# Rounding remainders of eight norms moved to GpSimd, three norms' squares summed whole, new order of the steps

## The chip, the cores and the metric

One Trainium2 chip, one core. The metric is the device time of one execution in microseconds. Five engines take part: TensorE (PE: matmuls, and its weight loads, PEld), VectorE (DVE), ScalarE (ACT), GpSimd (POOL) and SyncE (SP, which starts nearly all DMAs). Each works through its own list of instructions in order; semaphores tie them together.

## The reference

Two layers of a decoder with 528 tokens (16 learned ones and 512 of the input) of width 1024, in fp32. A layer is

```
a = rms_norm(h); proj = a @ w_in                    # columns for three groups of heads
DSA: q, k normed and rotated; an indexer's scores choose 128 keys per query; softmax over them
FoX: q, k normed; softmax of q k / 8 + c_q - c_k, c the running sum of log sigmoid of a gate
GLA: gated linear attention; decay from log_sigmoid((glr @ w2 + b)) / 16, summed in chunks;
     its output normed per head, times silu(gg)
h += concat(DSA, FoX, GLA) @ w_out
h += (silu(gate) * up) @ w_down, with gate, up = rms_norm(h) @ w_gate_up
```

`rms_norm(y) = y * rsqrt(mean(y*y) + eps) * gain`, over 64 or (GLA's output) 128 features. Features lie on the partitions here, so the sum of squares over a head is a product with a matrix of ones on PE.

## The kernel before

All products with weights are made from rounded halves: a weight unit (128 x 1024) comes by DMA to `raw`, ACT rounds it to `whi` (line 1099), POOL makes the remainder `wlo` (line 604), and PE adds whi*xhi, whi*xlo (lines 716, 807, 808) and wlo*xhi (lines 722, 813, the low pass). Each layer has 24 projection units, 8 of the output, 44 of gate and up, 24 of the way down.

While PE works on the 24 projection units, all engines also do the mixers. A step is one piece of this: `("proj", k, hf, p)` is a third of one half of unit k (DKIK, IQ, SMALL, DQ, FQ, FK, FV, GQ, GK, GV, GG name the units; p = 0 and 1 are the high passes over four tiles each, p = 2 is the low pass); `square` and `norm` with a unit are the two stages of a norm; `index`, `lowest`, `topk` and `select` choose the keys; `logits`, `turn`, `values`, `back`, `mixed` are attention for a group, a block and a head; `gla_att`, `gla_kv`, `gla_out` are the chunks of GLA. Steps of one kind have a fixed order among themselves (`chains_of_steps`). How the kinds are interleaved on each engine is written out by hand: `STEPS_OF` has a string of letters per layer and engine (A is a projection, B prenorm, C square, D norm, and so on), and `BANKS_OF` says in which of four PSUM banks each of PE's side jobs lies. An engine never takes steps in another order than its string, whatever is ready.

A norm of unit k goes so. ACT squares the features twice: whole to `sqb` (line 1166) and rounded to `sq_parts[:, 1]` (line 1167). DVE subtracts one from the other to `sq_parts[:, 0]` (line 1457), the remainder. PE multiplies both parts by ones, four matmuls of 266 columns (line 823). ACT makes Ln and Exp of the sums (lines 1139, 1175), DVE scales the features (lines 1445, 1448). The first seven norms (DKIK, DQ, DQ+1, FQ, FQ+1, FK, FK+1) come early in the mixers, the four of GLA's output (GV to GV+3) late. There is one set of square tiles, so ACT squares the next only when the sums of the last are made:

```
if n:
    wait_done(("norm", NORM_ORDER[n - 1]))
```

The gate of GLA is one step on DVE, `gate_log` (line 1487 on): one combination, ten running sums of a chunk each (line 1493), then the exponents' arguments. `turn_tile` of SMALL (line 846) transposes a unit for the heads. In layer 1 PE's first pieces (all of DKIK, and of IQ) are made ahead of the mixers' steps by `first_halves`, which leaves them out of the list. At the mixers' end `out` adds up the first output units: part 0 the GLA half, part 1 the attention half (line 716).

## Time and profile before

| | us |
|---|---|
| median of 3 runs | 1332.86 (1332.19 to 1334.34) |
| profiled execution | 1333.27 |
| its span | 1331.5 |
| PE busy | 1308.7 (98%) |
| DVE busy | 649.2 (49%) |
| ACT busy | 539.7 (41%) |
| POOL busy | 530.9 (40%) |

The span counts from the first instruction to the last; the execution's time has some 1.8 us around it. Busy time of PE is drawn with modelled ends that overlap the next matmul's start, so short waits do not show as idle time. The mixers of layer 0 lie between 25 and 256 us, those of layer 1 between 697 and 914 us.

### The profile page before, as it was taken

How to read it: one execution, taken by the hardware profiler on the slowest of the kernel's cores; microseconds unless marked ns; L12 is line 12 of the kernel's file. 1: busy time of each engine (PE TensorE's matmuls, PEld its weight loads, DVE VectorE, ACT ScalarE, POOL GpSimd, SP SyncE). 2: the span in 40 equal slices, each digit the busy share in tenths (PEclk: the TensorE clock that was granted, in tenths of full speed). 3: DMA queues.
4: the chain of work that ended last, by engine and by line, in shares of the span. 5: the costliest groups of instructions: out<-in, count | busy, mean ns of one | idle time of the engine just before them, and what ended most of it. 6: DMA issues, size and time to landing. Idle time of an engine off the chain costs nothing.

```text
span 1331.5 us, 22884 instructions
## 1 busy us (share of the span) xinstructions
PE 1308.7 (98%) x8678; PEld 1195.7 (90%) x8678; DVE 649.2 (49%) x1108; ACT 539.7 (41%) x874; POOL 530.9 (40%) x256
## 2 busy tenths in 40 slices
PE   7999999999999999999999999999999999999998
PEld 7999999999999999999998899987878888888887
DVE  4688988563333333322225999985643333331000
ACT  5566458543222222322235674385332222222221
POOL 2535311234444434444436342112444444444444
PEclk9999999999999999999999999999999999999999
DMA  5221210132222222222323212111222322223334
GB/s 185 89 81 55 80 33 32 33 111 80 95 94 79 94 95 81 92 95 98 106 80 94 80 67 67 33 48 48 95 83 93 94 94 94 95 95 104 102 99 153
DMA packets 33595, 114.11 MB, mean 86 GB/s; under 512 B 4352, under 2 KB 4736, under 8 KB 33536
## 3 DMA queue, kind: packets, MB, share of 16 engines
q1 hardware_dynamic: 32816, 112.23, 25.5%
q10 hardware_dynamic: 720, 1.09, 0.2%
q8 instruction: 38, 0.62, 0.2%
q14 instruction: 21, 0.17, 0.0%
HBM read 109.84 MB, written 2.10 MB: 84 GB/s over the span
## 4 chain that ended last, share of the span: by engine, by line
PE 52%; issue 32%; POOL 9%; DVE 5%; ACT 1%; DMA 1%; POOLq 0%; SPq 0%; DVEq 0%; ACTq 0%
PE ps L716 20%; PE ps L722 10%; POOL wlo L604 9%; PE ps L813 5%; PE ps L807 5%; PE ps L808 4%; PE ps L930 1%; PE ps L878 1%; PE ps L903 1%; PE ps L823 1%; PE ps L913 1%; PE ps L987 1%; DMA raw<-in_weights 1%; PE ps L773 1%; PE ps L969 1%
## 5 line engine op out<-in xcount | busy, mean ns | idle before, releaser
L604 POOL TENSOR_TENSOR wlo<-raw,whi 128x1024 fp32r<-128x1024 f32 x202 | 501.1, 2482 | 789.9 <-ACT whi L1099 789.6
L1099 ACT ACTIVATE whi<-raw 128x1024 fp32r<-128x1024 f32 x202 | 213.9, 1059 | 587.5 <-PE ps L722 549.1
L716 PE MATMUL ps<-xhi,whi 128*128 128x264 f32 (+1 forms) x1096 | 327.9, 322 | 7.2 <-ACT whi L1099 7.1
L716 PE MATMUL ps<-xlo,whi 128*128 128x264 f32 (+1 forms) x1096 | 326.6, 322 | 0.0
L716 PEld LDWEIGHTS ps<-xhi,whi 128*128 128x128 f32 x1096 | 206.8, 189 | 24.4 <-ACT whi L1099 6.8
L716 PEld LDWEIGHTS ps<-xlo,whi 128*128 128x128 f32 x1096 | 206.7, 189 | 16.1
L722 PE MATMUL ps<-xhi,wlo 128*128 128x264 f32 (+1 forms) x1096 | 195.4, 321 | 0.3 <-POOL wlo L604 0.2
L722 PEld LDWEIGHTS ps<-xhi,wlo 128*128 128x128 f32 x1096 | 162.9, 188 | 17.3 <-issue 1.0
L807 PE MATMUL ps<-xhi,whi 128*128 128x264 f32 (+1 forms) x632 | 176.3, 308 | 0.4 <-ACT whi L1099 0.3
L808 PE MATMUL ps<-xlo,whi 128*128 128x264 f32 (+1 forms) x632 | 171.1, 300 | 0.0
L716 PE MATMUL ps<-hlo,whi 128*128 128x264 f32 (+1 forms) x528 | 157.3, 321 | 0.0
L716 PE MATMUL ps<-hhi,whi 128*128 128x264 f32 (+1 forms) x528 | 157.2, 321 | 0.0
L1711 DVE TENSOR_TENSOR hid<-ps,rstd 128x528 f32<-128x528 f32 (+1 forms) x44 | 30.8, 700 | 213.1 <-PE ps L722 213.1
L807 PEld LDWEIGHTS ps<-xhi,whi 128*128 128x128 f32 x632 | 119.1, 188 | 5.6 <-issue 0.8
L808 PEld LDWEIGHTS ps<-xlo,whi 128*128 128x128 f32 x632 | 119.2, 189 | 3.5
L1726 DVE TENSOR_TENSOR h<-ps,h 128x528 f32<-128x528 f32 (+1 forms) x16 | 11.2, 700 | 204.3 <-PE ps L722 204.3
L716 PEld LDWEIGHTS ps<-hlo,whi 128*128 128x128 f32 x528 | 99.3, 188 | 7.9
L716 PEld LDWEIGHTS ps<-hhi,whi 128*128 128x128 f32 x528 | 99.2, 188 | 7.8
L1717 DVE TENSOR_TENSOR hlo<-hid,hhi 128x528 f32 (+1 forms) x44 | 82.9, 1883 | 41.1 <-ACT hhi L1372 41.1
L813 PE MATMUL ps<-xhi,wlo 128*128 128x264 f32 (+1 forms) x632 | 102.5, 304 | 0.0
L722 PE MATMUL ps<-hhi,wlo 128*128 128x264 f32 (+1 forms) x528 | 95.5, 321 | 0.0
L813 PEld LDWEIGHTS ps<-xhi,wlo 128*128 128x128 f32 x632 | 87.0, 188 | 4.3 <-issue 0.8
(196 smaller groups left out, 1696.1 us busy)
## 6 DMA issues: line engine op xcount, KB each, us to landing
raw<-in_weights SPq DMA_DIRECT2D x202, 512.0 KB, 3.5
out_hT<-h SPq DMA_DIRECT2D x8, 256.0 KB, 4.2
h<-in_hT SPq DMA_DIRECT2D x4, 264.0 KB, 6.4
h<-in_hT ACTq DMA_DIRECT2D x4, 264.0 KB, 6.0
cst<-in_consts SPq DMA_DIRECT2D x1, 780.5 KB, 9.3
xnb<-feat SPq DMA_DIRECT2D x20, 33.2 KB, 2.2
feat<-xnb SPq DMA_DIRECT2D x20, 33.2 KB, 2.0
cst<-in_consts SPq DMA_DIRECT2D x1, 532.0 KB, 4.5
```

Source lines behind the costliest of these rows:

```text
L604: nc.gpsimd.tensor_tensor(wlo[:, b], raw[:, b], whi[:, b].bitcast(F32), ALU.subtract).then_inc(split_done, 1)
L716: nc.tensor.matmul(bank(bank_no, cut.stop - cut.start), whi[:, b, k % KT], x(k)[t][:, cut], start=(first and k == ks[0] and t == 0), stop= ...
L722: ins = nc.tensor.matmul(bank(bank_no, cut.stop - cut.start), wlo[:, b, k % KT], x(k)[0][:, cut], start=False, stop=(last and k == ks[-1]))
L773: ins = nc.tensor.matmul(bank(b0 + hf, CUT), ones, square[:, cut], start=(k == 0), stop=(k == KT - 1))
L807: nc.tensor.matmul(o, whi[:, k % 2, n], xhi[:, n, cut], start=(n == 0), stop=False)
L808: nc.tensor.matmul(o, whi[:, k % 2, n], xlo[:, n, cut], start=False, stop=False)
L813: ins = nc.tensor.matmul(o, wlo[:, k % 2, n], xhi[:, n, cut], start=False, stop=(n == KT - 1))
L823: ins = nc.tensor.matmul(bank(b0 + hf, HALF), ones_r[:, at:at + 128], sq_parts[:, part, hf * HALF:(hf + 1) * HALF], start=(part == 0), sto ...
L878: ins = nc.tensor.matmul(ps[out_rows, at + a:at + z], q, kk[:, 2 * m + part, a:z], start=(part == 0), stop=(part == 1))
L1099: return nc.scalar.activation(whi[:, b], raw[:, b], ACT.Copy).then_inc(hi_done, 1)
L1711: nc.vector.tensor_tensor(tokens(l, hid[:, b]), wide(l, 4 * b + 2), tokens(l, rstd[:]), ALU.mult).then_inc(ev.acc_free, 1)
L1717: nc.vector.tensor_tensor(hlo[:, bass.ds(j * 2 + b, 1), of].rearrange("p a t -> p (a t)"), hid[:, b, of], hhi[:, bass.ds(j * 2 + b, 1), of ...
```

## The change

1. The norms of DKIK, DQ and DQ+1 keep one whole square in `sqb` (two tiles in turn) and PE sums it as plain fp32: two matmuls of 266 columns per norm, no rounded square, no remainder. ACT may square one norm ahead there.
2. For the other eight norms the remainder is made by POOL, with its own steps `square_parts` in POOL's list, between the weight units' subtractions; DVE has no square step any more.
3. `gate_log` is cut into `gate_log`, `gate_sum` (twice) and `gate_arg`, so that other steps can stand between them.
4. All strings of `STEPS_OF` and `BANKS_OF` are new, the DMA list's too.

```diff
+SPLIT_SQUARES = (FQ, FQ + 1, FK, FK + 1, GV, GV + 1, GV + 2, GV + 3)
...
+def square_step(k):
+    return ("square_parts" if k in SPLIT_SQUARES else "square", k)
...
-        "square": [("square", k) for k in NORM_ORDER],
+        "square": [square_step(k) for k in NORM_ORDER],
...
-        "gate": [("gate", 0), ("gate", 1), ("gate_log",), ("gate_exp",), ("decays",), ("turn_k", 0), ("turn_k", 1)],
+        "gate": [("gate", 0), ("gate", 1), ("gate_log",), ("gate_sum", 0), ("gate_sum", 1), ("gate_arg",),
+                 ("gate_exp",), ("decays",), ("turn_k", 0), ("turn_k", 1)],
...
-     POOLE: "AAQQAAAAAAAAAAQQQAAAAQAAAAAAAA",
...
+     POOLE: "AAQQAAAACACAQCAQACAQAAAAAQAAAAACCCCAAA",
...
+                def square(k):
+
+                    pool.wait_ge(ev.sq_whole, SPLIT_SQUARES.index(k) + 1)
+                    pool.wait_ge(ev.sq_ready, SQUARES[k] + 1)
+                    nc.gpsimd.tensor_tensor(sq_parts[:, 0], sqb[:, 0], sq_parts[:, 1].bitcast(F32), ALU.subtract).then_inc(ev.sq_split, 1)
...
-                    pe.wait_ge(ev.sq_split, SQUARES[k] + 1)
                     at = C_BLK - C_ONE if k < GV else 0
+                    if k in SPLIT_SQUARES:
+                        pe.wait_ge(ev.sq_split, SPLIT_SQUARES.index(k) + 1)
+                    else:
+                        pe.wait_ge(ev.sq_ready, SQUARES[k] + 1)
                     for hf in range(2):
-                        for part in range(2):
-                            ins = nc.tensor.matmul(bank(b0 + hf, HALF), ones_r[:, at:at + 128],
-                                                   sq_parts[:, part, hf * HALF:(hf + 1) * HALF], start=(part == 0), stop=(part == 1))
+                        half = slice(hf * HALF, (hf + 1) * HALF)
+                        if k in SPLIT_SQUARES:
+                            for part in range(2):
+                                ins = nc.tensor.matmul(bank(b0 + hf, HALF), ones_r[:, at:at + 128], sq_parts[:, part, half],
+                                                       start=(part == 0), stop=(part == 1))
+                        else:
+                            ins = nc.tensor.matmul(bank(b0 + hf, HALF), ones_r[:, at:at + 128].bitcast(F32),
+                                                   sqb[:, SQUARES[k] % 2, half], start=True, stop=True)
...
-                    if n:
+                    if k in SPLIT_SQUARES or n and NORM_ORDER[n - 1] in SPLIT_SQUARES:
                         wait_done(("norm", NORM_ORDER[n - 1]))
-                    elif l == 0:
+                    elif n >= 2:
+                        wait_done(("norm", NORM_ORDER[n - 2]))
+                    elif n == 0 and l == 0:
 
                         act.wait_ge(cst_loaded, 16)
                         act.wait_ge(ones_loaded, 16)
                         nc.scalar.activation(ones_r[:], cst[:, C_ONE:C_ROT], ACT.Copy).then_inc(ones_rounded, 1)
-                    nc.scalar.activation(sqb[:, 0], feat[:, place(k)], ACT.Square).then_inc(ev.sq_whole, 1)
-                    nc.scalar.activation(sq_parts[:, 1], feat[:, place(k)], ACT.Square).then_inc(ev.sq_ready, 1)
+                    if k in SPLIT_SQUARES:
+                        nc.scalar.activation(sqb[:, 0], feat[:, place(k)], ACT.Square).then_inc(ev.sq_whole, 1)
+                        nc.scalar.activation(sq_parts[:, 1], feat[:, place(k)], ACT.Square).then_inc(ev.sq_ready, 1)
+                    else:
+                        nc.scalar.activation(sqb[:, n % 2], feat[:, place(k)], ACT.Square).then_inc(ev.sq_ready, 1)
...
-                def square(k):
-                    n = SQUARES[k]
-                    dve.wait_ge(ev.sq_whole, n + 1)
-                    dve.wait_ge(ev.sq_ready, n + 1)
-                    nc.vector.tensor_tensor(sq_parts[:, 0], sqb[:, 0], sq_parts[:, 1].bitcast(F32), ALU.subtract).then_inc(ev.sq_split, 1)
...
-                    for t in range(2):
-                        for c in range(NB):
-
-                            of = feat[:, place(GG + 2 + t), block_of(c)]
-                            own[0] += 1
-                            nc.vector.tensor_tensor_scan(feat[:, place(GG + t), block_of(c)], of, of, 0.0, ALU.add,
-                                                         ALU.min).then_inc(ev.dve_step, 1)
+
+                def gate_sum(t):
+                    for c in range(NB):
+
+                        of = feat[:, place(GG + 2 + t), block_of(c)]
+                        own[0] += 1
+                        nc.vector.tensor_tensor_scan(feat[:, place(GG + t), block_of(c)], of, of, 0.0, ALU.add, ALU.min).then_inc(ev.dve_step, 1)
                     dve.wait_ge(ev.dve_step, own[0])
-                    b = chunks(e)
+
+                def gate_arg():
+                    b = chunks(feat[:, pair(GG)])
                     mid, end = b[:, :, :, BLK // 2 - 1], b[:, :, :, BLK - 1]
```

The order of instructions moves everywhere in the mixers. Three places:

POOL in layer 0, in the first half of the mixers; `wlo<-raw,whi` is a weight unit's remainder, `sq_parts` a norm's. Before:

```order
18 L623 COPY q_odd<-cst 4x532 x2
19 L604 TENSOR_TENSOR wlo<-raw,whi 128x1024 x10
20 L663 COPY k_fox<-feat 4x532 x4
21 L669 MEMSET feat 64x1064
22 L623 COPY feat<-cst 4x532 x2
23 L676 MEMSET feat 64x1064
24 L604 TENSOR_TENSOR wlo<-raw,whi 128x1024 x4
```

Now:

```order
18 L631 COPY q_odd<-cst 4x532 x2
19 L612 TENSOR_TENSOR wlo<-raw,whi 128x1024 x4
20 L695 TENSOR_TENSOR sq_parts<-sqb,sq_parts 128x532
21 L612 TENSOR_TENSOR wlo<-raw,whi 128x1024
22 L695 TENSOR_TENSOR sq_parts<-sqb,sq_parts 128x532
23 L612 TENSOR_TENSOR wlo<-raw,whi 128x1024
24 L671 COPY k_fox<-feat 4x532 x4
25 L695 TENSOR_TENSOR sq_parts<-sqb,sq_parts 128x532
26 L612 TENSOR_TENSOR wlo<-raw,whi 128x1024
27 L677 MEMSET feat 64x1064
28 L631 COPY feat<-cst 4x532 x2
29 L612 TENSOR_TENSOR wlo<-raw,whi 128x1024
```

The FoX remainders now stand one by one between the weight units; those of GLA come later, four in a row ahead of the last three units of the layer's projections (in layer 1 with one unit behind the first of them).

PE in layer 1, from the sums of norm GV+1 to those of norm GV+2 (`ps<-sq_parts` a norm's sums, `v_fox,probs_t` a head's values, `cst,probs` a head's transposes, `xhi,wlo` a low pass). Before:

```order
2405 L823 MATMUL ps<-sq_parts,ones_r 128x266 x4
2406 L945 MATMUL ps<-v_meta,p_meta_t 128x260
2407 L938 MATMUL ps<-cst,p_meta 128x128
2408 L813 MATMUL ps<-xhi,wlo 128x512 x8
2409 L930 MATMUL ps<-v_fox,probs_t 128x65 x3
2410 L913 MATMUL ps<-cst,probs 128x128 x3
2411 L930 MATMUL ps<-v_fox,probs_t 128x65 x3
2412 L913 MATMUL ps<-cst,probs 128x128 x3
2413 L823 MATMUL ps<-sq_parts,ones_r 128x266 x4
```

Now:

```order
2381 L842 MATMUL ps<-sq_parts,ones_r 128x266 x4
2382 L960 MATMUL ps<-cst,p_meta 128x128
2383 L952 MATMUL ps<-v_fox,probs_t 128x65 x3
2384 L935 MATMUL ps<-cst,probs 128x128 x3
2385 L952 MATMUL ps<-v_fox,probs_t 128x65 x3
2386 L827 MATMUL ps<-xhi,wlo 128x512 x8
2387 L842 MATMUL ps<-sq_parts,ones_r 128x266 x4
```

One head's transposes and the meta tokens' values have gone from between the two norms. A plain fp32 matmul (values, meta values) appears as two records in the trace, so that a row x3 makes six; a transpose and a matmul of rounded operands appear as one.

PE at the end of layer 1's mixers (`v_fox,probs_t` the last head's values, `v_meta` the meta tokens' part, `cst,o_tok` the transposes of finished heads, `mix_hi,whi` the output projection). Before:

```order
2460 L930 MATMUL ps<-v_fox,probs_t 128x65 x8
2461 L945 MATMUL ps<-v_meta,p_meta_t 128x260
2462 L954 MATMUL ps<-cst,o_tok 128x128 x2
2463 L716 MATMUL ps<-mix_hi,whi 128x512
2464 L716 MATMUL ps<-mix_lo,whi 128x512
```

Now:

```order
2472 L730 MATMUL ps<-mix_hi,whi 128x512
2473 L730 MATMUL ps<-mix_lo,whi 128x512
2474 L736 MATMUL ps<-mix_hi,wlo 128x512 x4
2475 L976 MATMUL ps<-cst,o_tok 128x128 x2
2476 L730 MATMUL ps<-mix_hi,whi 128x512
```

The last transposes have moved from ahead of the GLA half of the output projection to behind it (rows 2457 to 2474 of the new list), directly ahead of the attention half.

## Rows read from the trace of the kernel before

**Rows 1.** page, span and busy time of the engines
```profile
span 1331.5 us, 22884 instructions
PE 1308.7 (98%) x8678; PEld 1195.7 (90%) x8678; DVE 649.2 (49%) x1108; ACT 539.7 (41%) x874; POOL 530.9 (40%) x256
```

**Rows 2.** windows: mixers 0, output and feed-forward 0, mixers 1: length, busy us (count), clock
```profile
core 0: us, PE busy (x) PEld busy (x) DVE busy (x) ACT busy (x) POOL busy (x), PEclk, DMA share, GB/s
25.00:256.00 231.00, 225.46 (x1794) 216.50 (x1793) 183.96 (x432) 139.28 (x283) 76.12 (x49) 1.00 0.18 59
256.00:697.00 441.00, 440.72 (x3585) 439.13 (x3584) 149.72 (x143) 131.03 (x160) 187.79 (x76) 1.00 0.28 92
697.00:914.00 217.00, 211.29 (x1431) 190.68 (x1430) 179.75 (x397) 136.84 (x273) 74.23 (x49) 1.00 0.19 62
```

**Rows 3.** waits of PE, whole run: us in total, times, longest
```profile
PE ps L823 <- DVE sq_parts L1457: 4.8, 5, 1.2
PE ps L846 <- DVE feat L1435: 1.4, 2, 1.1
PE ps L716 <- DVE mix_lo L1635: 1.1, 1, 1.1
PE ps L954 <- DVE o_tok L1626: 1.0, 1, 1.0
```

**Rows 4.** timeline of PE: start, us, engine, line, what [idle before]
```profile
45.19 0.74 PE L846 MATMUL ps<-cst,feat 128*128 128x128 f32 x5 [1.06 <-DVE feat L1435]
...
57.42 0.74 PE L823 MATMUL ps<-sq_parts,ones_r 128*128 128x266 f32 x4 [0.55 <-DVE sq_parts L1457]
...
73.09 0.28 PE L808 MATMUL ps<-xlo,whi 128*128 128x264 f32 x1
74.56 0.73 PE L823 MATMUL ps<-sq_parts,ones_r 128*128 128x266 f32 x4 [1.18 <-DVE sq_parts L1457]
...
698.54 0.74 PE L823 MATMUL ps<-sq_parts,ones_r 128*128 128x266 f32 x4 [0.79 <-DVE sq_parts L1457]
...
733.12 0.73 PE L823 MATMUL ps<-sq_parts,ones_r 128*128 128x266 f32 x4 [1.22 <-DVE sq_parts L1457]
```

**Rows 5.** timeline of ACT and DVE ahead of two of these starts
```profile
69.21 0.64 ACT L1167 ACTIVATE sq_parts<-feat 128x532 fp32r<-128x532 f32 x1
73.70 0.71 DVE L1457 TENSOR_TENSOR sq_parts<-sqb,sq_parts 128x532 fp32r<-128x532 f32 x1
...
696.39 0.65 ACT L1166 ACTIVATE sqb<-feat 128x532 f32<-128x532 f32 x1 [0.98 <-DVE feat L1435]
697.68 0.71 DVE L1457 TENSOR_TENSOR sq_parts<-sqb,sq_parts 128x532 fp32r<-128x532 f32 x1 [1.32 <-ACT sq_parts L1167]
```

**Rows 6.** groups by form: busy us, mean ns of one, idle before
```profile
L1457 DVE TENSOR_TENSOR sq_parts<-sqb,sq_parts 128x532 fp32r<-128x532 f32 x22 | 16.7, 759 | 5.6 <-ACT sq_parts L1167 5.3
L604 POOL TENSOR_TENSOR wlo<-raw,whi 128x1024 fp32r<-128x1024 f32 x202 | 501.1, 2482 | 789.9 <-ACT whi L1099 789.6
```

**Rows 7.** timeline of PE: a norm's sums, and one head's fp32 logits
```profile
25.91 0.73 PE L823 MATMUL ps<-sq_parts,ones_r 128*128 128x266 f32 x4
26.48 0.29 PE L807 MATMUL ps<-xhi,whi 128*128 128x264 f32 x1
...
905.41 1.05 PE L903 MATMUL ps<-k_fox,q_odd 128*128 128x264 f32 x4
906.30 0.60 PE L913 MATMUL ps<-cst,probs 128*128 128x128 f32 x4
```

**Rows 8.** timeline of DVE and POOL, 41 to 47 us
```profile
41.91 2.79 DVE L1467 TENSOR_TENSOR xnb<-xnb 96x532 f32<-96x532 f32 x1
41.39 5.54 POOL L604 TENSOR_TENSOR wlo<-raw,whi 128x1024 fp32r<-128x1024 f32 x2
```

**Rows 9.** timeline, a GLA norm's sums and the next squares
```profile
203.79 0.74 PE L823 MATMUL ps<-sq_parts,ones_r 128*128 128x266 f32 x4
205.18 0.63 ACT L1167 ACTIVATE sq_parts<-feat 128x532 fp32r<-128x532 f32 x1
```

More of the change, by code:

```diff
@@ L239 @@
+    "23130120320320200203203020302301320",
 )
 ON = {
-    "prenorm": (PE, ACTE), "square": (ACTE, DVEE), "norm": (PE, ACTE, DVEE), "gather": (DMAE,),
-    "rope": (PE, DVEE), "spread": (DMAE,), "split_k": (ACTE, DVEE), "split_q": (ACTE, DVEE), "part": (ACTE,),
-    "even_q": (ACTE,), "turn_tile": (PE, ACTE), "index": (PE, ACTE, DVEE), "lowest": (DVEE,),
-    "select": (DVEE,), "topk": (DVEE,), "fox_log": (ACTE, DVEE), "gate": (PE, ACTE), "gate_log": (ACTE, DVEE),
+    "prenorm": (PE, ACTE), "square": (ACTE,), "square_parts": (ACTE, POOLE), "norm": (PE, ACTE, DVEE),
@@ L248 @@
+    "gather": (DMAE,), "rope": (PE, DVEE), "spread": (DMAE,), "split_k": (ACTE, DVEE),
+    "split_q": (ACTE, DVEE), "part": (ACTE,), "even_q": (ACTE,), "turn_tile": (PE, ACTE),
+    "index": (PE, ACTE, DVEE), "lowest": (DVEE,), "select": (DVEE,), "topk": (DVEE,), "fox_log": (ACTE, DVEE),
+    "gate": (PE, ACTE), "gate_log": (ACTE, DVEE), "gate_sum": (DVEE,), "gate_arg": (DVEE,),
     "gate_exp": (ACTE,), "decays": (DVEE,), "turn_k": (PE, ACTE), "masks": (POOLE,), "clear_fox": (POOLE,),
@@ L1342, in gla_mix @@
                     nc.scalar.activation(mix_hi[:, 4 + hd], feat[:, place(GG + hd)], ACT.Copy).then_inc(ev.gla_hi, 1)
-                do = dict(prenorm=prenorm, proj=proj, square=square, norm=norm, split_k=split_k, split_q=split_q_hi, part=part, even_q=even_q,
+                do = dict(prenorm=prenorm, proj=proj, square=square, square_parts=square, norm=norm, split_k=split_k, split_q=split_q_hi, part=part, even_q=even_q,
                           turn_tile=turn_tile,
@@ L1684, in gla_lo @@
                                             ALU.subtract).then_inc(ev.gla_split, 1)
-                do = dict(proj=proj, square=square, norm=norm, rope=rope, split_k=split_k, split_q=split_q_lo, gate_log=gate_log, fox_log=fox_log, decays=decays, index=index, topk=topk, lowest=lowest,
+                do = dict(proj=proj, norm=norm, rope=rope, split_k=split_k, split_q=split_q_lo, gate_log=gate_log, gate_sum=gate_sum, gate_arg=gate_arg,
+                          fox_log=fox_log, decays=decays, index=index, topk=topk, lowest=lowest,
                           select=select, logits=logits, scale=scale, mixed=mixed, gla_att=gla_att, gla_kv=gla_kv,
```

47 lines of the change are left out of this document (23 added, 24 removed).

## Prediction

> **What bounds the kernel now.** I read the page's busy shares first: TensorE (PE) is busy for 1308.7 of 1331.5 us, no other engine for more than half [rows 1]. The second view is the table of windows, since the change touches only the mixers [rows 2]. The reader is to see that the output and feed-forward stretch of layer 0 leaves PE 0.3 us idle in 441. The mixers leave 5.5 us in layer 0 (231.00 less 225.46) and 5.7 us in layer 1 (217.00 less 211.29), 11.2 together, while VectorE (DVE) is busy for 80 to 83% of them. The granted clock is 1.00, the 2.4 GHz level, throughout, so it has no term here. So the time can change in two ways: by the work on PE, and by those 11.2 us. Third, the list of PE's waits says what they are made of [rows 3]: five waits of a norm's sums (line 823) for DVE's remainder of line 1457 make 4.8 us, the largest item. The timeline shows three of them at the first three norms: 0.55 us at 57.42 (DQ, layer 0), 0.79 at 698.54 (DKIK, layer 1), 1.22 at 733.12 (DQ+1, layer 1), in sum 2.56 [rows 4]. The other two, 2.24 us, are FOX norms.
>
> A wait costs more than its idle time. At 73.09 the last matmul ahead of a wait starts; the norm starts 1.47 us later with 1.18 idle [rows 4]. Matmuls of this kind start 0.123 us apart (441 us through 3585 [rows 2]), though each is drawn 0.28 long. So the loss is 1.47 - 0.12 = 1.35, the idle time plus 0.16. The five cost 4.8 + 5 x 0.16 = 5.6 us.
>
> Durations come from the profiled execution, 1333.27 us (span 1331.5 and 1.8 around it); the median of the runs shown is 1332.86, 0.41 lower. The sum is made against the first and moved by 0.41 at its end.
>
> **1. The first three norms' squares are summed whole.** They are now plain fp32. PE's price is read from the FOX logits, which are plain fp32 too: line 903 issues two matmuls of 264 columns for a head, the trace draws four records, and they take from 905.41 to 906.30, 0.89 us. A norm's four rounded matmuls take from 25.91 to 26.48, 0.57 us [rows 7]. So each such norm costs 0.32 more, and 3 norms x 2 layers add **+1.9 us** on the engine that sets the time. Off PE go 6 remainders on DVE (6 x 0.76 = 4.6 us [rows 6]) and 6 second squares on ACT.
>
> Do the three waits go? At 698.54 PE had arrived 0.79 earlier, at 697.75. ACT's first square ends at 696.39 + 0.65 = 697.04 [rows 5], and this alone is now waited for: the wait goes. The piece that the new order puts behind this norm instead of ahead (pIQ) is in layer 1 already issued before the mixer's steps begin, so PE arrives no earlier. For DQ and DQ+1 the remainder is no longer behind DVE's queue either. Gain: 2.56 + 3 x 0.16 = **-3.0 us**.
>
> **2. FOX and GLA remainders by GpSimd (POOL).** 16 of them leave DVE (12.2 us) and come to POOL. POOL's subtraction of 1024 columns has a mean of 2.48 us [rows 6]; for 532 columns that makes an estimate of 2.48 x 532/1024 = 1.29 us, against 0.71 undisturbed on DVE. The bounds of a remainder's delay are 0.5 us later by that difference, and earlier by all that it stood in DVE's queue. The row at 74.56 shows how much that is: ACT's second square ended at 69.21 + 0.64 = 69.85, DVE began the remainder at 73.70, 3.85 us later, since the selection's steps stood ahead of it [rows 5]. I take the earlier side for the two FOX waits, because POOL is busy for only a third of the mixers (76 of 231 us [rows 2]) and 3.85 is more than its longer subtraction: **-2.6 us** (2.24 + 2 x 0.16). For the GLA norms I take 0; they show no wait now, and what covers them is told under the second rival.
>
> Each remainder that waits on POOL holds up the weight splits queued behind it. The first extract shows one split between every two FOX remainders. A unit's split is needed only a unit later on PE (48 matmuls, 5.9 us at 0.123), against 1.29 us more for each: cost 0 while that cover stands; without it PE waits at its low pass (line 813).
>
> The Trainium skill, page "SBUF — State Buffer", section "Who interferes with whom", calls the port pair that DVE and GpSimd share an exclusive lock held for a whole instruction. What the trace shows of it goes into the sum by itself: at 41.91 DVE's addition of two SBUF tiles took 2.79 us, while POOL had two subtractions running from 41.39 [rows 8]; undisturbed remainders of like size take 0.71. So the 20.6 us of POOL (16 x 1.29) give part of DVE's relief back. I count the relief of DVE as no gain on PE beyond the waits named.
>
> **3. The steps of the gate** run the same instructions, in three steps instead of one. Their cost is 0; before, ten scans stood in a row on DVE, and now projections' evictions go between them.
>
> **4. The new order.** In layer 0 the turn of SMALL waited 1.06 us for DVE (45.19 [rows 4]); it now comes three pieces later (24 matmuls, 2.9 us), so the wait goes: **-1.2 us**. At layer 1's end the transpose of the last heads waited 1.02 us for DVE [rows 3]. Now the GLA half of the output projection stands between (third extract). But then the attention half follows that transpose directly, as layer 0 has it, where it waited 1.1 us for the last mix_lo [rows 3]: one for the other, 0. All other steps move as well, the gates and projections forward, layer 0's attention back. New waits cannot be read from the old trace. Their bounds are 0 and the 11.2 us that the mixers show now, if the new order were twice as bad; I take **+1.5 us**, nearer to 0, because what is left of 11.2 once the waits named (4.8, 1.06) are gone is spread over small ones. The place that I expect first is FQ's norm in layer 0. It follows the last index queries closely, and two squares on ACT, a 1.29 us remainder and perhaps a running split lie between.
>
> **Sum:** +1.9 - 3.0 - 2.6 - 1.2 + 1.5 = -3.4 us, 1329.9 for a profiled execution, **1329.5 us** as a median. What a measurement of this kernel tells from no change is about 0.2%, 2.7 us.
>
> **Rivals.** *The lock eats the relief (no change).* The Trainium skill, page "Perfetto Trace Analysis", section "Optimizing Scalar/DVE Operations", says that moving work between DVE and GpSimd might not help, because they share an SBUF port. As a mechanism of this kernel: POOL's 20.6 us stand against the 16.7 us of remainders that DVE loses [rows 6]; if each of them stopped DVE, DVE would be 3.9 us slower. The row at 41.91 speaks for it; against it, MAX and MATCH_REPLACE, most of DVE's work in the selection, read one tile each. Then the two FOX waits stay or come back elsewhere (no -2.6) and half of the 3.9 reaches PE: +1.9 - 3.0 - 1.2 + 1.5 + 1.9 = +1.1, a median of 1334.0.
>
> *The GLA norms starve (slower).* They are a chain: sums on PE, two squares on ACT, the remainder, the next sums. From the start of one norm's sums to the end of the second square are 2.02 us (203.79 to 205.18 + 0.63 [rows 9]), with 1.29 and 0.2 for hand-overs 3.5 us. In layer 1, between GV+1 and GV+2, the second extract leaves PE 24 records, at a mean of 0.152 (217 us through 1431 [rows 2]) 3.6 us, and the norm's own 0.57: some 0.7 us of cover. A split running on POOL (2.4 us), a DVE operation holding the port, or late squares use it up, and all steps behind the norm wait on PE. If each of the eight GLA norms came 1.2 us after its cover, that is 8 x 1.36 = 10.9 us in place of the 1.5: +6.0, a median of 1338.9. It decides from 7.6 us of new waits on (4.9 gained above, and 2.7). Against it: before, the same norms had no wait, and POOL's splits are sparse there.
>
> *The change does not do what it says:* the waits for remainders were DVE's lateness in general and show up at the next wait on DVE. Then only +1.9 is sure and the rest is exchanged: 1332 to 1335.
>
> **How the numbers follow.** The forecast has 0.50, the lock 0.28, the starving GLA norms 0.17, the exchange 0.05. The forecast's own range is 1325.5 (new waits 0 and 2.5 us more of the small waits gone by DVE's relief: -4.9 - 2.5) to 1331.5. The 8 in 10 range reaches over the second case and leaves out most of the third and the best luck: 1325.5 to 1335.5. Faster by over 0.2% (under 1330.2): 0.50. Within: 0.33. Slower: 0.17.
>
> **What would show it.** Right: in the list of PE's waits no entry of the first three norms, FOX norms under 0.5 us each, PE idle in the two mixers at 7 to 9 us instead of 11.2, fp32 sums of about 0.89 us per norm, and POOL remainders of 1.2 to 1.4 us. Wrong: PE waiting for POOL's sq_parts in the GLA stretch (third case); DVE's two-input operations longer than now, with its busy time down by less than 10 us (second case); a low pass of a projection waiting for wlo (the cover of part 2). The forecast falls if the mixers' PE idle stays at 11 us or more.

## Result: slower, 1336.82 us, and the profile after

The changed kernel takes 1336.82 us in the median of 9 runs (1334.77 to 1338.72), beside 1332.78 for the kernel before (9 runs, same chip): ratio 1.0027, 95% interval [1.0019, 1.0035], so 4.0 us slower, beyond the 2.7 us that I called measurable. The profiled execution took 1338.72 us, 5.45 more than that of before. The page after, against [rows 1]:

```profile
span 1336.9 us, 22872 instructions
PE 1315.5 (98%) x8678; PEld 1202.0 (90%) x8678; DVE 636.8 (48%) x1086; ACT 537.0 (40%) x868; POOL 549.9 (41%) x272
...
PEclk9989999999999999999999999999999999999999
```

DVE has 12.4 us less work and POOL 19.0 more, as the change says. The new thing is in the line of the granted clock: its third slice is an 8. The windows that answer [rows 2] say where:

```profile
25.00:256.00 231.00, 227.57 (x1760) 217.19 (x1759) 176.86 (x419) 137.16 (x280) 83.09 (x57) 0.98 0.17 56
256.00:697.00 441.00, 439.70 (x3587) 438.44 (x3586) 149.76 (x143) 129.42 (x157) 188.64 (x77) 1.00 0.28 93
697.00:914.00 217.00, 212.24 (x1428) 192.76 (x1427) 172.47 (x383) 135.43 (x267) 85.03 (x57) 1.00 0.18 61
```

PE's idle time seems to go from 11.2 to 8.2 us (3.43 and 4.76), inside my 7 to 9. But both mixers now end later, and the wait at the end of each has slipped out of its window:

```profile
260.12 0.36 PE L730 MATMUL ps<-mix_hi,whi 128*128 128x264 f32 x1 [1.02 <-DVE mix_lo L1655]
...
924.67 0.49 PE L730 MATMUL ps<-mix_hi,whi 128*128 128x512 f32 x1 [0.93 <-DVE mix_lo L1655]
```

With these two the bracketed waits of PE's timeline from 25 us on come to 10.1 us (3.37 + 1.02 + 4.76 + 0.93), beside 10.8 before (5.27 + 5.57): 0.8 less, not 3. And PE's busy time in layer 0 rose by 2.1 us while 34 fewer matmuls lie in the window. In windows of 2 us (length, busy us of PE, its weight loads, DVE, ACT and POOL with counts, then the clock):

```profile
84.00:86.00 2.00, 2.00 (x19) 2.00 (x17) 1.93 (x3) 0.39 (x1) 0.51 (x1) 1.00 0.00 0
86.00:88.00 2.00, 1.30 (x6) 0.66 (x4) 1.90 (x7) 1.32 (x3) 1.88 (x3) 1.00 0.00 0
88.00:90.00 2.00, 1.14 (x8) 1.03 (x8) 1.90 (x7) 1.95 (x3) 1.86 (x3) 1.00 0.00 0
90.00:92.00 2.00, 1.82 (x10) 1.75 (x10) 1.86 (x7) 1.84 (x3) 2.00 (x2) 0.66 0.03 8
92.00:94.00 2.00, 2.00 (x8) 1.54 (x8) 1.90 (x5) 0.66 (x2) 1.88 (x3) 0.50 0.30 47
...
98.00:100.00 2.00, 2.00 (x11) 2.00 (x11) 1.45 (x5) 1.97 (x2) 1.03 (x1) 0.50 0.57 168
100.00:102.00 2.00, 2.00 (x15) 2.00 (x15) 0.11 (x1) 1.35 (x3) 0.00 (x0) 0.78 0.23 94
102.00:104.00 2.00, 2.00 (x19) 2.00 (x18) 1.93 (x5) 0.00 (x0) 0.00 (x0) 1.00 0.00 0
```

From 90 to 102 us the mean clock is 0.66, four times 0.50 and 0.78: PE runs at 1.2 GHz instead of 2.4. The work missing is 2 x (0.34 + 4 x 0.50 + 0.22) = **5.1 us**. The matmul of the output projection that waits for the last mix_lo, at the end of the mixers of layer 0, starts at 254.62 us before and at 260.12 after: 5.5 later. From there to the end of the span it is 1076.9 and 1076.8 us. So all of the loss lies in layer 0, and nearly all of it is this stretch. Ahead of it, PE's timeline:

```profile
85.08 1.13 PE L827 MATMUL ps<-xhi,wlo 128*128 128x264 f32 x8
86.14 1.16 PE L888 MATMUL ps<-feat,par_all 16*128 16x266 f32 x4
88.86 0.39 PE L821 MATMUL ps<-xhi,whi 128*128 128x264 f32 x1 [1.56 <-ACT whi L1121]
...
90.28 0.93 PE L842 MATMUL ps<-sq_parts,ones_r 128*128 128x266 f32 x4 [0.18 <-POOL sq_parts L695]
91.01 0.42 PE L821 MATMUL ps<-xhi,whi 128*128 128x264 f32 x1
91.23 0.42 PE L822 MATMUL ps<-xlo,whi 128*128 128x264 f32 x1
```

The gate's product (line 888: four narrow matmuls, 16 rows), a gap of 1.56 us, eight matmuls, and then matmuls start 0.22 us apart instead of 0.12. The gap is a wait for ACT to round the weights of FV. Why ACT is late is read back along three engines (POOL, then DVE, then ACT):

```profile
76.59 1.40 POOL L695 TENSOR_TENSOR sq_parts<-sqb,sq_parts 128x532 fp32r<-128x532 f32 x1 [5.46 <-ACT sq_parts L1192]
77.95 2.46 POOL L612 TENSOR_TENSOR wlo<-raw,whi 128x1024 fp32r<-128x1024 f32 x1
85.50 3.23 POOL L671 COPY k_fox<-feat 4x532 f32<-4x532 f32 x4 [5.08 <-issue]
88.81 1.33 POOL L695 TENSOR_TENSOR sq_parts<-sqb,sq_parts 128x532 fp32r<-128x532 f32 x1
```

```profile
76.43 0.37 DVE L1608 SCALAR_TENSOR_TENSOR score<-score,top 128x144 f32<-128x144 f32 x1
76.83 1.33 DVE L1609 SCALAR_TENSOR_TENSOR score<-score,top 128x144 f32<-128x144 f32 x1
78.19 2.38 DVE L1610 SCALAR_TENSOR_TENSOR score<-score,causal 128x144 f32<-128x144 f32 x1
...
86.21 0.77 DVE L1462 TENSOR_TENSOR feat<-ps,rstd 128x264 f32<-128x264 f32 x2
```

```profile
86.68 0.65 ACT L1191 ACTIVATE sqb<-feat 128x532 f32<-128x532 f32 x1 [2.29 <-DVE feat L1462]
87.23 0.63 ACT L1192 ACTIVATE sq_parts<-feat 128x532 fp32r<-128x532 f32 x1
87.77 1.04 ACT L1121 ACTIVATE whi<-raw 128x1024 fp32r<-128x1024 f32 x1
```

POOL's remainder and the weight split right behind it hold two small DVE operations for 1.33 and 2.38 us; the one ahead of them, of the same shape, took 0.37. In layer 1 the second of them took 0.31 undisturbed. That is 3 us of DVE, of which some 2 are new: the eight DVE instructions of this select took 3.45 us in the kernel before (70.22 to 73.67), one of them stretched to 1.14 us beside a weight split, and take 5.63 here (74.94 to 80.57). DVE then takes unit FK.1 out of PSUM only at 86.21, behind a top-k round, the forget gate's logs and norm FQ1. ACT's squares of FK wait 2.29 us for it, and the rounding of FV's weights stands behind those squares. So the first theory was **clock**: a gap of PE's work brings the fall, and this chain brings the gap. Its rivals: the **price of the edits** (they cost this wherever they stand), and the **order** (the new order loses on PE whatever the clock does).

### The profile page after: what moved, and what is told of

Same layout as the page of the kernel before. It is cut to its first block, busy times and chain, and to the rows that moved or that the text cites. A ratio compares the mean times of both kernels' runs of the same rounds, so it can differ in the third digit from the quotient of the medians.

```text
span 1336.9 us, 22872 instructions
## 1 busy us (share of the span) xinstructions
PE 1315.5 (98%) x8678; PEld 1202.0 (90%) x8678; DVE 636.8 (48%) x1086; ACT 537.0 (40%) x868; POOL 549.9 (41%) x272
## 4 chain that ended last, share of the span: by engine, by line
PE 51%; issue 31%; POOL 9%; DVE 6%; ACT 1%; DMA 1%; POOLq 0%; SPq 0%; DVEq 0%; ACTq 0%
PE ps L730 20%; PE ps L736 10%; POOL wlo L612 9%; PE ps L821 4%; PE ps L827 4%; PE ps L822 4%; PE ps L952 1%; PE ps L900 1%; PE ps L925 1%; PE ps L935 1%; DVE score L1569 1%; PE ps L787 1%; DMA raw<-in_weights 1%; PE ps L1009 1%; DVE feat L1472 1%
## 5 line engine op out<-in xcount | busy, mean ns | idle before, releaser
L1747 DVE TENSOR_TENSOR h<-ps,h 128x528 f32<-128x528 f32 (+1 forms) x16 | 11.2, 699 | 204.3 <-PE ps L736 204.3
```

## The experiments

Orders are given by step names; pFK.1c is the last piece of FK's second weight unit (on ACT the rounding of the unit two further on, on DVE the taking out of PSUM, on POOL a weight split). Each time is a median beside the kernel before on the same chip, whose medians were 1332.97 to 1333.32.

### 1. Two links of the chain, one at a time

```diff
 e1: after, ACT, layer 0
-square_parts:FK  pFK.1c
+pFK.1c  square_parts:FK
 e2: after, DVE, layer 0
-topk:2,0  fox_log  norm:FQ1  pFK.1c
+pFK.1c  topk:2,0  fox_log  norm:FQ1
```

> The changed kernel with one pair of ScalarE steps exchanged in layer 0: the rounding of unit FV's weights goes ahead of the squares of norm FK, so that it does not stand behind DVE's late sum of unit FK.1. In the changed kernel's trace TensorE waits 1.56 us for this rounding at 88.9 us and the granted clock is then 0.50 from 92 to 100 us and 0.66 and 0.78 beside that, about 10 us at 1.2 GHz that cost some 5 us. Theory 'clock': TensorE's gap at 86 to 89 us shrinks, the stretch at 1.2 GHz goes or shrinks, the mean clock comes out at 0.998 to 1.000 instead of 0.996, and the time falls by 3 to 5.5 us to 1331 to 1334. Rival 'price of the edits' (whole fp32 sums and GpSimd's slower remainders cost the time wherever they stand): the time stays within 1 us of 1336.8. Rival 'order': PE loses the time at other waits, and the clock's dip only moves to another place: 1335 to 1338 with the clock still 0.996.

> The same gap attacked from its other end: the changed kernel with DVE's sum of unit FK.1 ahead of the first top-k round (and so ahead of the forget gate's log and norm FQ1's apply, which it stood behind until 86.2 us although TensorE had ended the unit near 80.3). ScalarE's squares of FK then no longer wait for it, and neither does the rounding of FV behind them. Theory 'clock': the same gain as in the run with ScalarE's pair exchanged, 3 to 5.5 us, with a mean clock of 0.998 to 1.000; norm FQ1's apply comes up to 1 us later, which may cost up to 0.5. Rival 'price of the edits': within 1 us of 1336.8. If only one of the two runs recovers the clock, the gap has a second cause than the chain from DVE's sum over the squares to the rounding.

Measured: 1338.57 us (ratio 1.0033 [1.0021, 1.0045]), clock 0.996, and 1339.06 (1.0042 [1.0029, 1.0056]), 0.995. Neither recovers anything. In e1 the wait for the rounding is gone, and at the next norm stands another:

```profile
90.40 0.93 PE L842 MATMUL ps<-sq_parts,ones_r 128*128 128x266 f32 x4 [1.79 <-POOL sq_parts L695]
```

In e2 it is 2.11 us at the same norm FK. The gap has a second cause, which the first had covered: the new order puts POOL's four copies for the forget sums (3.23 us from 85.50, above) ahead of the remainder of FK. That rules out the chain as I had told it, not yet the clock.

### 2. The parts of the change without its order

e3 is the new code with the order and banks of before (gate steps together, remainders on POOL behind the weight splits beside them). e4 is the kernel before with the first three norms summed whole, remainders on DVE. It is not that part quite alone: its code also has the gate in steps, which stand side by side in DVE's list, as in e3. So e3 and e4 differ only in who makes the eight remainders.

```diff
 e4, DVE, both layers
-square:DKIK  square:DQ  square:DQ1
 (the eight others stay)
```

> The changed kernel's code (first three norms' squares summed whole, eleven remainders on GpSimd, the gate's sums in steps) in the order of steps and banks of the kernel before; the remainders stand in GpSimd's order behind the weight step that precedes them in time, and the three gate steps stand together where the one step stood. Theory 'clock and order': the edits themselves are worth -2 to +1 us, so 1331 to 1334 with a clock of 1.00. Rival 'price of the edits': they cost what the changed kernel lost, 1335.5 to 1338. A third possibility is a new wait on GpSimd's remainders, since the old order was not made for them: then PE's idle rows name L842 <-POOL with over 2 us and the time is 1334 to 1337 with the clock at 1.00.

> The kernel before with one part of the change alone: the squares of the first three norms (DKIK, DQ, DQ1) are summed whole in fp32, the other eight remainders stay on DVE where they were, order and banks are those of before. From the prediction: +1.9 us of TensorE for the fp32 sums against -3.0 us of its waits for DVE's remainders, so -1.1 +- 0.7: 1331 to 1332.5. If fp32 sums cost more than the 0.3 us each over the rounded ones, or the wait for DVE is replaced by one for ScalarE's squares, it is 1333 to 1334.5. Theory 'price of the edits' needs at least +1 us here or in the run with GpSimd's remainders in the old order.

Measured: e3 1333.06 (0.9996 [0.9987, 1.0005]); e4 1332.10 (0.9991 [0.9982, 1.0000]). The price of the edits falls as a theory: all of them together cost at most 0.7 us in the old order, by the interval. e4 comes out at -1.2 where -1.1 was forecast for this part; its interval reaches to no change, but its trace agrees, with 8.2 us of bracketed waits in the mixers where the kernel before has 10.8.

### 3. Which layer's order

e8: layer 0 in the old order and banks, layer 1 in the new one.

> The changed code with layer 0 in the old order of steps and banks (as in the run with the old order throughout) and layer 1 in the new one. Theory 'clock': the loss lies in layer 0 alone, so this gives 1331 to 1333.5 (the old order throughout gave 1333.06) with no fall at 90 us; from the idle time in the mixers of layer 1 (4.8 us in the changed kernel, 4.5 in the old order throughout) the new order of layer 1 should be worth nothing or up to +0.5 us. Rival 'order': the new order of layer 1 costs too, 1334.5 or more.

Measured: 1332.63 (1.0000 [0.9991, 1.0009]), clock 1.000 in the profiled execution. The loss is layer 0's order; layer 1's costs nothing in the median. Two of the eleven executions took 1335.40 and 1335.57 at a mean clock of 0.997, so in some of them the clock falls with this order too.

### 4. All waits of that place at once

```diff
 e5: e1, and POOL, layer 0
-pFQ1.1c  spread_sums  square_parts:FK  pFK.1c  clear_even
+pFQ1.1c  square_parts:FK  pFK.1c  spread_sums  clear_even
 e6: e5 and e2
 e11: after, POOL, layer 0: spread_sums, clear_even, clear_gla_even behind pFV1.1c
 e12: e11 and e1 and e2
```

> The changed kernel with both waits of the stretch at 86 to 91 us attacked in one: ScalarE's exchange of the first experiment, and on GpSimd the four copies for the forget sums (3.2 us from 85.5 us) behind the weight step of FK.1 instead of ahead of the remainder of FK. In the first experiment TensorE's wait for the rounding went and one of 1.79 us for that remainder came in its place (GpSimd had the copies in hand until 88.7), the clock fell as before, and the time was 1338.6. Theory 'clock' as it now stands (any gap of some 1.6 to 2.1 us here, next to the gate's small matmuls, is followed by the fall to 1.2 GHz): the wait at norm FK shrinks to 0.7 us or less, the fall goes, mean clock 0.999 to 1.000, time 1331 to 1334. Rival 'order' (the light matmuls of gate and norm at 86 to 91 us bring the fall without any wait): gap small and the clock still falls, 1336 to 1338.

> As the run beside it, and DVE's sum of unit FK.1 ahead of the first top-k round too, so that the squares of FK start some 3 us sooner on ScalarE and GpSimd's remainder is ready before TensorE asks for it. Theory 'clock': no wait over 0.3 us between 86 and 91 us, no fall of the clock, 1331 to 1333.5, not slower than the run beside it. Rival 'order': the clock falls although there is no wait, 1336 to 1338.

Measured: e5 1340.83 (1.0059 [1.0045, 1.0073]), e6 1339.97 (1.0048 [1.0034, 1.0062]). Both miss their numbers, and show where the wait goes. Windows and timeline of e6:

```profile
86.00:88.00 2.00, 2.00 (x12) 1.44 (x11) 1.93 (x5) 1.81 (x4) 1.12 (x1) 1.00 0.00 0
88.00:90.00 2.00, 2.00 (x18) 1.95 (x16) 1.86 (x7) 1.92 (x3) 2.00 (x2) 1.00 0.04 8
90.00:92.00 2.00, 2.00 (x12) 1.48 (x11) 1.86 (x7) 1.36 (x3) 1.81 (x4) 1.00 0.21 39
...
100.00:102.00 2.00, 1.36 (x6) 1.39 (x7) 1.81 (x5) 0.13 (x1) 0.50 (x1) 0.69 0.43 172
102.00:104.00 2.00, 2.00 (x11) 2.00 (x11) 0.66 (x1) 1.97 (x3) 0.00 (x0) 0.50 0.00 0
```

```profile
100.64 1.13 PE L842 MATMUL ps<-sq_parts,ones_r 128*128 128x266 f32 x4 [3.33 <-POOL sq_parts L695]
```

The gate's two products and norm FK pass at 86 to 92 us without a gap, and the clock holds at 1.00. Now PE comes to norm FK1 3.33 us before POOL's remainder, which stands behind the copies and two clears, and the clock falls there. The gap moved and the fall moved with it (in e5: a gap of 3.75 us up to 102.40, in which the clock falls at 101.6).

Both runs, and e2, have a second fall, in layer 1, of 1.7 us by the windows. It begins within 1.4 us of the start of the gate's second product there, ahead of which PE waits 0.51 to 0.52 us. In e6:

```profile
765.00 1.13 PE L888 MATMUL ps<-feat,par_all 16*128 16x266 f32 x4 [0.51 <-DVE stat L1634]
766.00:768.00 2.00, 2.00 (x11) 1.94 (x11) 1.86 (x7) 1.74 (x2) 1.50 (x1) 0.59 0.10 39
```

The profiled executions of the changed kernel and of e1 have the same product at 764.6 to 764.7 with 0.52 and 0.53 us ahead of it, and no fall. So a stretch of this kind can bring the fall and need not.

> The changed kernel with GpSimd's order alone changed in layer 0: the copies for the forget sums and the two clears stand behind the weight step of FV1.1 again, as in the old order, and no longer between the remainders; the remainders of FK and FK1 so come free of them. TensorE's wait for the rounding of FV at 88.9 us (1.56 us, from DVE's late sum through ScalarE's squares) is not touched. Theory 'wait': that gap stays near 1.6 us, so the fall stays, 1335.5 to 1338. If GpSimd's order is the whole cause: clock 1.00 and 1331 to 1334.

> All three waits of layer 0's new order taken away: ScalarE's rounding of FV ahead of the squares of FK, DVE's sum of FK.1 ahead of the first top-k round, and GpSimd's copies and clears behind the weight step of FV1.1. With the first two and the copies only one place later the gap at 89 us was gone, the clock held there, and a new wait of 3.3 us for the remainder of FK1 at 100.6 us brought the fall instead (1339.97). Theory 'wait': no gap over 1.2 us between 75 and 110 us, no fall, mean clock 0.999 to 1.000, time 1331 to 1333.5. Rival 'order': falls again at some other place or PE loses 3 us in small waits, 1335 or more.

Measured: e11 1335.29 (1.0019 [1.0010, 1.0028]), clock 0.998: the gap is 1.55 us as said, and the fall behind it costs 1.7 us by its windows instead of 5.1. e12's profiled execution keeps the clock at 1.000 and takes 1335.67; its other four take 1335.94 to 1338.65, two of them at 0.997, so in some of them the clock falls somewhere, and the median is 1337.90 (1.0035 [1.0021, 1.0048]). I expected 1331 to 1333.5. PE has new waits at other places in e12, the longest 1.67 us for POOL's weight split at 118.36 and 0.98 for a rounding at 114.48. So even without a fall this order is 2.4 us behind (1335.67 against the 1333.27 of before, one execution each), and by e8 the loss is layer 0's: the theory "order" is right for this part.

### 5. What brings the fall

e7 takes the narrow product away and leaves the wait. e9, e10, e13 and e14 put a gap into the kernel **before**, alone: ACT squares DQ n times more, into the same buffer with the same values.

```diff
 e7: after, PE and ACT, layer 0
-gate:0  pFV.0a  norm:FK  pFV.0b  gate:1
+pFV.0a  norm:FK  pFV.0b  gate:0  gate:1
 e9, e10, e13, e14: before, ACT, square(k), n = 2, 3, 4, 6
+if l == 0 and k == DQ:
+    for _ in range(n):
+        own[0] += 1
+        nc.scalar.activation(sqb[:, 0], feat[:, place(k)], ACT.Square).then_inc(ev.act_step, 1)
+        act.wait_ge(ev.act_step, own[0])
 e18: e13, and PE, layer 0: gate:0 right ahead of norm:DQ (ACT's gate:0 behind split_q:2)
```

> The changed kernel with its waits left alone and the first of the gate's two small products (16 rows, 4 matmuls, 1.1 us) moved from ahead of the waited piece to beside the second, behind norm FK. TensorE then reaches the piece of unit FV some 1 us sooner and waits longer for it: a gap of 2 to 2.7 us with full matmuls in front. Theory 'wait' (the idle time brings the fall): the clock falls at 88 to 91 us as before, mean 0.995 to 0.997, 1336 to 1339. Theory 'light work' (the small matmuls beside the gap bring it): the clock stays or its fall is shorter, 1332 to 1335.

Measured: 1339.56 (1.0049 [1.0035, 1.0063]). The gap became 2.67 us at 88.66, with full matmuls ahead of it, and the clock fell (0.50 in 90:92). Narrow work is not needed for that. It fell again at 96.6, behind both of the gate's products, the second with a gap of only 0.80 us ahead of it.

> The kernel before, with one thing added: in layer 0 ScalarE squares DQ two times more (the same values into the same buffer, 0.65 us each) ahead of the two squares that norm DQ needs. Nothing of the output changes. TensorE's wait ahead of norm DQ (0.55 us at 57.4 us in the kernel before) becomes about 1.85 us; there is no gate product or other narrow matmul within some us of it but one pair of 128x144. Theory 'wait': a gap of this length is enough for the granted clock to fall to 1.2 GHz for some 8 to 10 us, so +1.3 us for the wait and +4 to +5 for the clock: 1337 to 1340. Theory 'light work' (it needs the small matmuls beside the gap): +1.3 to +2.5 us only, 1334 to 1336, clock 1.000.

> As the run beside it with three squares more, so a gap of about 2.5 us. Theory 'wait': the fall is there for certain, 1338 to 1341. If the shorter gap brings no fall and this one does, the length of the gap decides; if neither does, idle time alone is not what brings it: 1335 to 1337.

Measured: 1333.82 (1.0004 [0.9994, 1.0014]) and 1334.38 (1.0010 [1.0000, 1.0019]); no fall, but the gaps came out at 0.74 and 1.36 us, not 1.85 and 2.5: the first extra squares were partly hidden, why I did not trace. They decide nothing about 2 us. So two more:

> The kernel before with four more squares of DQ on ScalarE in layer 0 (same values, same buffer) ahead of those that norm DQ needs. Two and three of them made the gap ahead of norm DQ 0.74 and 1.36 us, so some 0.62 us each: about 2.0 us now. Theory 'wait': the fall of the granted clock follows it as it followed the gaps of 1.56 to 3.75 us in the changed order, some 4 us more in time: 1337.5 to 1340, mean clock 0.997. Rival 'wait alone is not enough' (it also takes the narrow gate products or further gaps close by): the time goes on as with two and three squares (1333.8, 1334.4), so 1335 to 1336, clock 1.000.

> As the run beside it with six more squares: a gap of about 3.2 us. Theory 'wait': a fall in every execution, 1339 to 1342, mean clock 0.996 to 0.997. Rival: 1336 to 1337.5 with the clock at 1.000. If this one falls and the run beside it does not, the length from which a gap decides lies between 2.0 and 3.2 us here and is shorter beside the gate.

Measured: e13 1335.72 (1.0019 [1.0010, 1.0028]), e14 1337.81 (1.0034 [1.0023, 1.0045]). First the row of e13 and its window, then those of e14:

```profile
58.37 0.73 PE L823 MATMUL ps<-sq_parts,ones_r 128*128 128x266 f32 x4 [2.10 <-DVE sq_parts L1462]
...
60.00:62.00 2.00, 2.00 (x19) 2.00 (x18) 1.94 (x4) 1.95 (x3) 0.00 (x0) 1.00 0.00 0
```

```profile
60.67 1.22 PE L823 MATMUL ps<-sq_parts,ones_r 128*128 128x266 f32 x4 [3.46 <-DVE sq_parts L1462]
...
60.00:62.00 2.00, 1.33 (x6) 1.36 (x7) 1.85 (x5) 1.72 (x4) 0.00 (x0) 0.52 0.03 8
```

In these executions a gap of 3.46 us alone brings the fall (0.52 in 60:62: it begins at 60.1, in the gap itself) and one of 2.10 does not. Other executions differ: the seven of e14 reach from 1339.38 us at a mean clock of 0.997 to 1335.91 at 1.000, the ten of e13 from 1334.75 at 1.000 to 1337.09 at 0.997. Their mean clock does not say where it fell: the profiled e13, at 0.999, has a fall of 1.7 us at the end of layer 1's mixers (914.9 to 918.3), where nothing was changed. In the changed kernel 1.56 us seems to be enough in nearly every execution: eight of the nine have 0.996 or 0.997, the fastest (1334.77) 0.999. e18 asks whether the gate's product takes part:

> As the run with four more squares of DQ (gap of 2.10 us ahead of norm DQ, no fall of the clock behind it, 1335.7), with the first gate product (4 matmuls of 16 rows, 1.1 us) moved from its place at 117 us to right in front of that norm, so that it stands beside the gap as in the changed kernel (where 1.56 us were enough). It takes some 0.5 to 1 us of the gap's time, so the gap is 1.1 to 1.6 us and the time without a fall 1334.5 to 1336. Theory 'gap and narrow products together': the clock falls at 60 us in most executions, +3 to +5 us: 1338 to 1340, mean clock 0.997. Rival 'the gap alone counts': no fall, since the gap is shorter than the one that brought none, clock 0.999 to 1.000.

Measured: 1338.39 (1.0039 [1.0025, 1.0052]), 2.7 us above e13.

```profile
57.73 1.45 PE L864 MATMUL ps<-feat,par_all 16*128 16x266 f32 x4 [1.41 <-ACT relu L1280]
60.18 1.26 PE L821 MATMUL ps<-sq_parts,ones_r 128*128 128x266 f32 x4 [1.00 <-ACT feat L1222]
58.00:60.00 2.00, 1.18 (x4) 0.39 (x3) 1.85 (x5) 1.95 (x4) 0.00 (x0) 0.62 0.07 29
60.00:62.00 2.00, 1.82 (x8) 1.82 (x9) 1.03 (x2) 0.59 (x2) 0.00 (x0) 0.50 0.03 8
```

The fall is there, with no single gap over 1.41 us. The product waited for its bank, so the idle time is in two parts, 1.41 + 1.00. But the fall does not need the second part: 0.62 in 58:60 with 0.50 behind it puts its start at 60 - 2 x 0.76 = 58.5 us, while the product was running (57.73 to 59.18). Ahead of it lie 1.41 us without work and 0.8 of the narrow product, less idle time than the 2.10 us of e13 that brought no fall. In layer 0 of e6 the same product has no gap beside it and no fall. My reading, which fits these runs and which e18 supports without proving it: what counts is a stretch in which the array has little to do, gaps and narrow products together. What it does not explain is why the same stretch brings the fall in one execution and not in another, as in layer 1 of e6 and e1. That the fall is in part chance in each execution is a rival that e13 and e18 do not exclude, though all five executions of e18 are at 0.997 to 0.999 and the ten of e13 at 0.997 to 1.000.

### 6. The new order with the remainders on DVE

e15: after, with the eight remainders back on DVE, each where ACT's squares should be ready.

> The changed kernel, its order and banks, with the eight remainders of the FoX and GLA norms back on DVE (each put where ScalarE's squares are ready); the whole sums of the first three norms and the gate's steps stay. Theory 'GpSimd' (the new order fails because GpSimd holds the shared port while DVE is due and comes late with remainders): DVE is back in time, the gaps of 86 to 91 us shrink under 1.2 us, no fall, 1331 to 1334. Rival 'order' (TensorE reaches unit FV before DVE and ScalarE are through whatever GpSimd does; DVE has 2.8 us more work in front): the gap stays at 1.5 us or grows, with the fall, 1336 to 1340.

Measured: 1351.25 (1.0146 [1.0130, 1.0161]), far beyond either number. PE waits 2.98 us for the rounding of FV at 90.53 (1.56 in the changed kernel), up to 2.11 for remainders in both layers and 2.79 for another step of DVE at 902.27, with three falls of the clock, 6.8 us by the windows. With the remainders at these places DVE has no room for their 12 us in the new order. How much of the 14 us over the changed kernel is my choice of places, and so whether POOL is needed there, was not tried.

### 7. A version that beats both

e16 and e17 are e4 with two more norms summed whole: FQ1 in layer 0 and FK in layer 1 (e16), FQ in layer 0 and FQ1 in layer 1 (e17).

```diff
 e17
-SPLIT_SQUARES = (FQ, FQ + 1, FK, FK + 1, GV, ...)
+SPLIT_SQUARES = ((FQ + 1, FK, FK + 1, GV, ...),
+                 (FQ, FK, FK + 1, GV, ...))
```

> The kernel with whole squares alone (1332.1) with two more norms summed whole in fp32: FQ1 in layer 0 and FK in layer 1, the two at which TensorE still waits for DVE's remainder (0.70 us at 73.8, 1.06 us at 749.0). By the terms so far +0.33 us each for the fp32 sums, and up to -1.76 for the waits: -1.1 +- 0.6, so 1330.5 to 1331.8. If ScalarE's squares and not the remainders are what is late, the waits stay at half and the time is 1331.8 to 1332.5.

> The kernel with whole squares alone (1332.1), with FQ in layer 0 and FQ1 in layer 1 summed whole too: the trace of the run with FQ1 and FK shows that the waits of 0.70 us at 74.0 and of 1.06 us at 749.8 belong to these two. +0.33 us each for the fp32 sums, -1.76 at most for the waits: -1.1 +- 0.5, so 1330.5 to 1331.6. If it comes out at 1332 to 1333, the waits are gone and the time is lost behind them, at DVE's or ScalarE's steps that TensorE then reaches sooner.

Measured: e16 1332.43 (1.0000 [0.9991, 1.0009]): no gain, and its trace still had both waits, 0.70 and 1.06 us: I had named the wrong norms. e17 **1331.00** (0.9984 [0.9975, 0.9993]), the fastest here: 2.1 us below the kernel before and below the changed one, whose own ratio is 1.0027. Both waits for remainders are gone; the largest entry of PE's list in the mixers is now the turn of SMALL, in both layers:

```profile
PE ps L861 <- DVE feat L1455: 1.9, 2, 1.1
```

## Why the prediction was wrong

Forecast 1329.5, range 1325.5 to 1335.5, with 0.17 for slower; it came out slower and above the range.

**The step that failed** is the sentence "The granted clock is 1.00, the 2.4 GHz level, throughout, so it has no term here." It is true of the kernel before and says nothing of the one after: a new wait costs its own length and, where the clock falls with it, more: 5.1 us here, 1.7 to 5.1 in the experiments. My own sum had new waits of 1.5 us, all at face value. The other terms against the runs: the waits gone and new were to give -3.0 - 2.6 - 1.2 + 1.5 = -5.3 and give -0.8; the fp32 sums were to cost 1.9 and cost 0.9. So -0.8 + 0.9 + 5.1 = +5.2, against 5.45 measured. The clock alone would have left me at +1.7, 1335.0 in a profiled execution; the second error is that the waits came back elsewhere almost in full.

**Part 1, whole sums.** Mechanism right, price too high. The rows that answer [rows 7]:

```profile
24.86 1.06 PE L845 MATMUL ps<-sqb,ones_r 128*128 128x266 f32 x4
25.56 0.61 PE L827 MATMUL ps<-xhi,wlo 128*128 128x264 f32 x2
```

A norm takes 0.70 to 0.78 us from its start to the next, 4.3 for the six, not 0.89 each, so they cost +0.9 and not +1.9. The logits were the wrong row to take it from. The waits named went, except one: in the new order DQ still waits 0.89 us, now for ACT's square. In the old order all three went (e4), and the part did about what was forecast there (-1.2).

**Part 2, remainders on POOL.** The duration was near (1.37 us in the mean, 1.29 estimated):

```profile
L695 POOL TENSOR_TENSOR sq_parts<-sqb,sq_parts 128x532 fp32r<-128x532 f32 x16 | 22.0, 1372 | 75.9 <-ACT sq_parts L1192 75.8
```

But of the -2.6 only half came: FQ's wait in layer 0 (1.18 us) went, that of FQ1 in layer 1 (1.06) stayed, 1.03 at 754.25, now for POOL, which could start only when ACT's second square was there (752.71) and then took 1.40. In the old order the kernel with POOL's remainders (e3) is 1.0 us behind the one with DVE's (e4; nothing else differs), which is about as much as the intervals can tell. In the new order PE's list has these:

```profile
PE ps L730 <- DVE mix_lo L1655: 2.0, 2, 1.0
PE ps L821 <- ACT whi L1121: 1.6, 1, 1.6
PE ps L842 <- POOL sq_parts L695: 1.2, 2, 1.0
PE ps L900 <- DVE mix_hi L1500: 1.1, 1, 1.1
PE ps L845 <- ACT sqb L1194: 0.9, 1, 0.9
PE ps L854 <- DMA xnb<-feat: 0.8, 1, 0.8
```

The first error was to argue with POOL's mean load ("busy for only a third"). Two POOL instructions back to back held DVE for 3 us (above). The Trainium skill, page "SBUF — State Buffer", section "Who interferes with whom", says that a DVE instruction with two SBUF inputs contends with a GpSimd instruction that reads SBUF; the trace agrees, with 0.37 us for the first of the two (line 1589, kernel before) and 0.31 for the second alone, and 1.33 and 2.38 beside it. The second: I took POOL's other steps (copies, clears) as staying where they were. The diff of POOL's string was in front of me, and I costed only the splits.

**Part 3, gate in steps.** They are four steps, not three. Not tried by itself; it is in e3, e4, e16 and e17, and none of them is slower than the kernel before.

**Part 4, new order.** The turn of SMALL lost its wait, as said. Layer 1's end exchanged 1.02 us for 0.55 and 0.93, near the 0 that I took. "New waits" of 1.5 us was the wrong size and the wrong place: I expected them first at FQ's norm, which has none in layer 0. New are those at the rounding of FV (1.56) and at FK (0.18), and in layer 1 at 741.58 (0.76), 757.11 (1.14) and 764.63 (0.52): 4.2 us, where I took 1.5. Three old ones stayed or grew, with another releaser or later in the list: DQ in layer 0 (0.55, now 0.89), FQ1 in layer 1 (above), and the turn of SMALL in layer 1 (0.30, now 0.76 at 781.26). Some small ones of before are gone in return.

**The rivals.** The GLA norms do not starve: PE's list has two waits for sq_parts, both of FoX norms, so my slower case came true in its sign and not in its mechanism. The lock does act, but through one late link and not as an even tax. "The change does not do what it says", to which I gave 0.05, describes the waits best: new ones all but replace those removed, and in layer 1 the time did not move. It missed the clock as the forecast did.

**Still open.** The ledger misses the measurement by some 0.3 us. Where the clock falls in the slower executions of e12 is not known, since only one was profiled. The gate's cut was not tried by itself. Why the fall comes in some executions and not in others is not known.

## What to carry to other kernels

Where TensorE is the bound and runs at 2.4 GHz, judge a new order by its longest stretch of little work and not by the sum of its waits: the changed kernel waits 0.8 us less in its mixers and takes 4 us more. When removing one wait only uncovers the next, as three times here, the engine has been moved ahead of its suppliers, and the order is to be undone rather than mended. Try the parts of a change in the old order first: two runs showed here that the edits were sound and the order was not, and the whole sums, spread to the two norms that waited, beat both kernels (e17, with the gate in steps).

## What the runs showed of the hardware that I had not expected

- The price of a gap is not in proportion to its length. The fall that belongs to it in layer 0 cost, by the windows, 1.7 us (e6, e11, twice in e7), 3.4 (e5, e14, e18) or 5.1 (the changed kernel, e1, e2), with no order by the gap: 3.33, 1.55, and 2.67 and 0.80; 3.75, 3.46 and 1.41 + 1.00; 1.56, 1.79 and 2.11 us.
- It varies between executions of one kernel. The mixers of layer 1 end in gaps of 1.02 and 0.17 us around a narrow transpose in the kernel before and in e3 alike. In the profiled execution of before the clock stayed at 1.00 behind them; in that of e3 it fell (0.69, 0.50 and 0.96 from 912 to 918 us), some 1.7 us, and so it did there in those of e4, e13 and e17. Differences of up to 1.7 us between single executions of these kernels can be this alone.
- Plain fp32 sums are cheaper than their records suggest: four records of 0.39 us each, but 0.70 to 0.78 us from the first to the next work.
